# Experts of a mixture-of-experts layer: from rows kept apart and summed last, to scatters that add into one row per token

## The reference

```python
scores = sigmoid(t @ w_router)                 # 512 x 64
idx    = grouped top-8 of (scores + b_router)  # 8 experts for each token
gate   = sel / sum(sel) * 2.5
# each (token, expert) pair: rows are sorted by expert and padded to blocks
yb     = (silu(xb @ we_gate[e]) * (xb @ we_up[e])) @ we_down[e]    # D -> 256 -> D
y      = yb[dest] * gate
routed = segment_sum(y, tok)                   # the token's 8 rows are added
shared = (silu(t @ ws_gate) * (t @ ws_up)) @ ws_down
y      = routed + shared
x      = x + gt2 * rmsnorm(y, norm_ffn_post)
```

## Time and profile before

| | us |
|---|---|
| median of 3 runs | 1432.51 (1430.16 to 1439.59) |
| the profiled execution, own time | 1433.78 |
| its span, first to last instruction | 1431.9 |
| experts: first scatter to last | 680.7 to 1366.2 |
| combine: first load to end | 1380.1 to 1431.9 |

### The profile page before, as it was taken

The page is one execution under the profiler, slowest core; times in us unless marked ns, Lnnn a source line. Parts: engine busy times, 40 slices in busy tenths (PEclk is TensorE's granted clock), DMA queues, the critical chain, the costliest instruction groups (busy, mean ns, idle before and its releaser), DMA issues. The chain is left out here.

```text
span 1431.9 us, 18788 instructions
## 1 busy us (share of the span) xinstructions
PE 1314.6 (92%) x5765; PEld 912.0 (64%) x5765; DVE 1017.3 (71%) x1656; ACT 617.0 (43%) x944; POOL 254.3 (18%) x329
## 2 busy tenths in 40 slices
PE   5989999878798999986999999999999999999937
PEld 2666887637696444545767677777777676767613
DVE  4768988899633533536888888888888888887617
ACT  3421322263233103124656565665656565656402
POOL 0000000033000000002223232323232232332200
PEclk9999999988898999997999999999999999999969
DMA  9656244100004711325999999999999999988268
GB/s 331 214 206 235 67 169 147 52 22 1 1 1 184 265 59 78 157 90 213 339 343 364 351 355 353 352 344 357 382 389 351 350 342 345 362 323 322 107 239 355
DMA packets 86737, 340.80 MB, mean 238 GB/s; under 512 B 16982, under 2 KB 22296, under 8 KB 59556
## 3 DMA queue, kind: packets, MB, share of 16 engines
q1 hardware_dynamic: 66832, 306.51, 57.2%
q0 software_dynamic: 19584, 33.60, 6.4%
q10 hardware_dynamic: 276, 0.11, 0.0%
HBM read 333.87 MB, written 44.04 MB: 264 GB/s over the span
## 5 line engine op out<-in xcount | busy, mean ns | idle before, releaser
L2251 DVE TENSOR_TENSOR gate_up_low<-gate_up,gate_up_high 128x1024 fp32r<-128x1024 f32 x204 | 244.8, 1221 | 42.3 <-ACT gate_up_high L2142 36.3
L2223 PE MATMUL py<-down_ring,hT 128*128 128x512 f32 x544 | 250.0, 602 | 0.9 <-ACT hT L2161 0.9
L2184 PE MATMUL p_gate_up<-gate_up_high,x_hi 128*128 128x512 f32 x544 | 242.6, 446 | 5.3 <-DVE x_lo L2260 5.3
L2184 PE MATMUL p_gate_up<-gate_up_low,x_hi 128*128 128x512 f32 x544 | 216.8, 399 | 0.0
L2184 PE MATMUL p_gate_up<-gate_up_high,x_lo 128*128 128x512 f32 x544 | 215.7, 397 | 0.0
L2142 ACT ACTIVATE gate_up_high<-gate_up 128x1024 fp32r<-128x1024 f32 x204 | 203.6, 1051 | 0.7 <-PEq L1407 0.7
L2223 PEld LDWEIGHTS py<-down_ring,hT 128*128 128x128 f32 x544 | 98.0, 190 | 98.8 <-issue 98.7
L2184 PEld LDWEIGHTS p_gate_up<-gate_up_high,x_hi 128*128 128x128 f32 x544 | 104.0, 191 | 44.8 <-issue 21.1
L2184 PEld LDWEIGHTS p_gate_up<-gate_up_high,x_lo 128*128 128x128 f32 x544 | 103.7, 191 | 30.0 <-issue 10.9
L2113 POOL TENSOR_TENSOR carrier<-offsets 1x1 f32<-1x1 f32 x136 | 29.8, 219 | 521.6 <-DVE tokens L2269 474.1
L460 PE MATMUL pz<-h_hi,w_hi 128*128 128x512 f32 x288 | 116.9, 406 | 1.7 <-DVE ring_lo L537 1.7
(11 more groups left out here) (367 smaller groups left out, 1945.6 us busy)
## 6 DMA issues: line engine op xcount, KB each, us to landing
down_ring<-in_we_down SPq DMA_DIRECT2D x68, 1024.0 KB, 9.5
gate_up<-in_we_gate SPq DMA_DIRECT2D x51, 1024.0 KB
gate_up<-in_we_up SPq DMA_DIRECT2D x51, 1024.0 KB
ring<-in_w_ada SPq DMA_DIRECT2D x12, 2048.0 KB, 8.6
x_again<-in_we_gate SPq DMA_DIRECT2D x17, 1024.0 KB
x_again<-in_we_up SPq DMA_DIRECT2D x17, 1024.0 KB
ring<-in_w_in SPq DMA_DIRECT2D x8, 2048.0 KB, 8.3
rows<-expert_rows SPq DMA_DIRECT2D x6, 2048.0 KB, 19.0
```

The source lines that it names most:

```text
L2184: mm = pe.matmul(pgu[u % 2][:, :], x[:, u % 2, k, :], weights, start=(k == 0 and n == 0), stop=(k == KD - 1 and n == 2))
L2223: mm = pe.matmul(py[half][:, :], hT[:, u % 2, k, :], weights[:, k, half * N:half * N + N], start=(k == 0), stop=(k == 1))
L2251: V.tensor_tensor(moe.low[u % RING][:, :, piece(i), :], moe.gate_up[u % RING][:, :, piece(i), :], exact(w_hi[:, u % 2, :, piece(i), :]), A ...
```

## The change

- The scratch tensor of 4096 rows becomes `expert_sums` with one row per token (512 x 1024). At the start of the experts stage SP stores `moe.shared` (2 MB) to it.
- The scatter of each block adds to the token's row in HBM (`compute_op=ALU.add`), with the token's number as the row's number.
- Two blocks can hold the same token, so scatters go one at a time: Pool waits until scatter b-1 has landed before it issues scatter b, in every block.
- The row numbers and ranks fall away: the table has two values rather than three, `numbers` multiplies 6 columns rather than 9.
- `combine` loads 512 rows (2 MB) in four DMAs; the sums on TensorE and DVE are gone. Gate and squares work on whole tiles of 1024 columns.

```diff
@@ tabulate @@
-                for t in range(NT):
-                    link.sign(V.tensor_tensor_scan(rank[:, t, :], keep.ones[:, 0:NE], sel[:, t, :], 0.0, ALU.mult, ALU.add))
...
-                link.sign(V.tensor_tensor(rank, rank, sel, ALU.subtract))
...
-                for t in range(NT):
-                    link.sign(V.tensor_scalar(values[:, t, :, 2], rank[:, t, :], tokf[:, 2, t:t + 1], None, ALU.add))
-                link.wait()
@@ plan_experts @@
-    moe.parts = m.sb("table_parts", [P, NT, NE, 3, 3], BF16)
+    moe.parts = m.sb("table_parts", [P, NT, NE, 2, 3], BF16)
-    moe.rows = nc.dram_tensor("expert_rows", (S * TOPK, D), F32, kind="Internal").ap()
+    moe.sums = nc.dram_tensor("expert_sums", (S, D), F32, kind="Internal").ap()
@@ experts, sync @@
+            sp.wait_ge(s_x, 1)
+            sp.dma_start(moe.sums.rearrange("(t p) d -> p t d", p=P), moe.shared[:, :, :]).then_inc(s_start, 16)
             for u in range(RING):
                 weights(RING + u, u)
@@ experts, gpsimd @@
                 pool.wait_ge(s_rows, b + 1)
                 pool.wait_ge(s_yA, b + 1)
                 pool.wait_ge(s_yV, b + 1)
+                if isinstance(b, int) and b == 0:
+                    pool.wait_ge(s_start, 16)
+                else:
+                    scattered(pool, b - 1, (u + 3) % 4)
                 carry_wait(s_scatter, b, 1)
-                pool.indirect_dma_start(moe.rows, bass.IndirectOffsetOnAxis(row_ids[:, u % 4, 0:1], 0), y[:, u % 2, :], None,
-                                        bounds_check=last_row, oob_is_err=False).then_inc(s_out[u % 2], 16)
+                pool.indirect_dma_start(moe.sums, bass.IndirectOffsetOnAxis(row_ids[:, u % 4, 0:1], 0), y[:, u % 2, :], None,
+                                        bounds_check=last_token, oob_is_err=False,
+                                        compute_op=ALU.add).then_inc(s_out[u % 2], 16)
@@ experts, vector @@
-                V.tensor_tensor(row_ids[:, u % 4, :], number[:, u % 4, 2:3], moe.offsets[:, 1:2], ALU.add).then_inc(s_rows, 1)
+                V.tensor_tensor(row_ids[:, u % 4, :], number[:, u % 4, 1:2], moe.offsets[:, 0:1], ALU.add).then_inc(s_rows, 1)
@@ combine @@
+            for t in range(NT):
+                sp.dma_start(y[:, t, :], moe.sums[t * P:(t + 1) * P, :]).then_inc(s_in[t], 16)
...
+                act.activation(sq[:, :], y[:, t, :], ACT.Square, accum_out=total[:, t:t + 1]).then_inc(s_sq, 1)
+                act.wait_ge(s_sq, t + 1)
+                act.activation(mean[:, t:t + 1], total[:, t:t + 1], ACT.Copy, bias=D * RMS_EPS).then_inc(s_whole, 1)
...
+            def gated(t):
+
+                dve.wait_ge(s_in[t], 16)
+                V.scalar_tensor_tensor(out=scaled[:, t, :], in0=y[:, t, :], scalar=D ** 0.5, in1=keep.gate2[:, :],
                                        op0=ALU.mult, op1=ALU.mult).then_inc(s_gt, 1)
...
+            gated(0)
+            for t in range(NT):
+                if t + 1 < NT:
+                    gated(t + 1)
                 finish(t)
```

More of the change, by code:

```diff
@@ L1399 @@
 MAXB = NE + S * TOPK // P - 1
-NO_TOKEN, NO_ROW = 8 * S, 16 * S * TOPK
+NO_TOKEN = 8 * S
 BIG = 1e30
@@ L1433, in merge_route @@
         g8 = old(NT, NG, 8)
-        scores, biased, sel, gated, left, rank = (old(NT, NE) for _ in range(6))
-        values = old(NT, NE, 3)
+        scores, biased, sel, gated, left = (old(NT, NE) for _ in range(5))
+        values = old(NT, NE, 2)
         gs, top4, top8 = (old(NT, 8) for _ in range(3))
         gleft, gmask = old(NT, NG), old(NT, NG)
-        total, over, tokf, pf, bf = old(NT), old(NT), old(3, NT), old(1), old(4)
+        total, over, tokf, pf, bf = old(NT), old(NT), old(2, NT), old(1), old(4)
         before = old(P)
@@ L1528, in _ @@
             pool.memset(moe.offsets[:, 0:1], float(NO_TOKEN)).then_inc(s_io, 1)
-            pool.memset(moe.offsets[:, 1:2], float(NO_ROW)).then_inc(s_io, 1)
             for j in range(2 * NT):
@@ L1786, in _ @@
             link.sign(V.tensor_scalar(tokf[:, 1, :], tokf[:, 0, :], float(-NO_TOKEN), None, ALU.add))
-            link.sign(V.tensor_scalar(tokf[:, 2, :], tokf[:, 0, :], float(TOPK), float(-NO_ROW), ALU.mult, ALU.add))
             dve.wait_ge(s_x, 16)
@@ L1947, in plan_experts @@
     moe.n_blocks = m.sb("n_blocks", [1, 1], I32)
-    moe.offsets = m.sb("offsets", [P, 2])
+    moe.offsets = m.sb("offsets", [P, 1])
     moe.xg = m.sb("xg", [P, 4, D])
@@ L1978, in experts @@
         hot = m.sb("hot", [P, 2, NT, P], BF16)
-        column = m.sb("column", [P, 2, NT, 9], BF16)
-        number = m.sb("number", [P, 4, 3])
+        column = m.sb("column", [P, 2, NT, 6], BF16)
+        number = m.sb("number", [P, 4, 2])
         tokens = m.sb("tokens", [P, 4, 1], U32)
@@ L2009, in experts @@
         s_out = [m.sem(f"p5_scattered{i}") for i in range(2)]
+        s_start = m.sem("p5_sums_started")
         block = stack.enter_context(nc.Block())
@@ L2106, in _ @@
         def _(pool):
-            last_token, last_row = pool.to_reg(S - 1), pool.to_reg(S * TOPK - 1)
+            last_token = pool.to_reg(S - 1)
             def carry_wait(semaphore, b, place):
@@ L2211, in numbers @@
                 for t in range(NT):
-                    mm = pe.matmul(pid[:, 0:9], hot[:, u % 2, t, :], column[:, u % 2, t, :], start=(t == 0), stop=(t == NT - 1))
+                    mm = pe.matmul(pid[:, 0:6], hot[:, u % 2, t, :], column[:, u % 2, t, :], start=(t == 0), stop=(t == NT - 1))
                 mm.then_inc(s_id, 1)
@@ L2266, in numbers @@
                 taken(dve, s_x, b, 4)
-                V.tensor_reduce(number[:, u % 4, :], pid[:, 0:9].rearrange("p (v j) -> p v j", j=3), AX.X, ALU.add).then_inc(s_sum, 1)
+                V.tensor_reduce(number[:, u % 4, :], pid[:, 0:6].rearrange("p (v j) -> p v j", j=3), AX.X, ALU.add).then_inc(s_sum, 1)
                 dve.wait_ge(s_sum, b + 1)
@@ L2299, in combine @@
         m = Memory(nc, stack)
-        H = TOPK // 2
-        rows = m.sb("rows6", [P, NT, TOPK, D])
         x1 = moe.x1
         y, scaled = m.sb("y6", [P, NT, D]), m.sb("scaled6", [P, NT, D])
[L2304 to L2314, removed]
+        sq = m.sb("sq6", [P, D])
+        total, mean, rstd = m.sb("total6", [P, NT]), m.sb("whole6", [P, NT]), m.sb("rstd6", [P, NT])
+        s_in = [m.sem(f"p6_sums{t}_in") for t in range(NT)]
+        s_gt, s_sq, s_whole, s_r = m.sem("p6_y_gated"), m.sem("p6_squared"), m.sem("p6_squares"), m.sem("p6_rstd")
         s_o, s_st = m.sem("p6_out"), m.sem("p6_stored")
-        s_a = m.sem("p6_scalar_chain")
         block = stack.enter_context(nc.Block())
-        expert_rows = moe.rows.rearrange("(t p j) d -> t p j d", p=P, j=TOPK)
-        LAST = NT - 1
         def cols(half):
@@ L2337, in _ @@
             sp.wait_ge(s_st, 16 * 2 * NT)
[L2339 to L2348, removed]
         @block.gpsimd
@@ L2353, in _ @@
                 pool.wait_ge(s_whole, t + 1)
-                pool.tensor_tensor(rstd[:, t:t + 1], whole[:, t:t + 1], keep.power[:, 0:1], ALU.pow).then_inc(s_r, 1)
+                pool.tensor_tensor(rstd[:, t:t + 1], mean[:, t:t + 1], keep.power[:, 0:1], ALU.pow).then_inc(s_r, 1)
         @block.scalar
         def _(act):
-            link = Link(act, s_a)
             for t in range(NT):
-                act.wait_ge(s_y, 2 * t + 1)
+                act.wait_ge(s_in[t], 16)
                 if t:
[L2362 to L2368, removed]
+                    act.wait_ge(s_sq, t)
+                act.activation(sq[:, :], y[:, t, :], ACT.Square, accum_out=total[:, t:t + 1]).then_inc(s_sq, 1)
+                act.wait_ge(s_sq, t + 1)
+                act.activation(mean[:, t:t + 1], total[:, t:t + 1], ACT.Copy, bias=D * RMS_EPS).then_inc(s_whole, 1)
         @block.vector
@@ L2395, in gated @@
                                        op0=ALU.mult, op1=ALU.mult).then_inc(s_gt, 1)
             def finish(t):
+                dve.wait_ge(s_gt, t + 1)
                 dve.wait_ge(s_r, t + 1)
                 for half in range(2):
-                    dve.wait_ge(s_gt, 2 * t + half + 1)
                     V.scalar_tensor_tensor(out=x1[:, t, cols(half)], in0=scaled[:, t, cols(half)], scalar=rstd[:, t:t + 1],
                                            in1=x1[:, t, cols(half)], op0=ALU.mult, op1=ALU.add).then_inc(s_o, 1)
[L2405 to L2411, removed]
-                finish(t)
@@ L2413, in _ @@
-            for half in range(2):
-                dve.wait_ge(s_dve_in[LAST + half], 16)
-                tree(LAST, cols(half))
-                add(LAST, half)
-            for half in range(2):
-                gated(LAST, half)
-            finish(LAST)
+            gated(0)
+            for t in range(NT):
+                if t + 1 < NT:
+                    gated(t + 1)
+                finish(t)
 class Names:
```

## The result

The changed kernel took **1461.88 us** (median of 4, 1458.94 to 1473.06) against 1434.2 us for the kernel before, run beside it (median of 4): ratio 1.0205, 95% interval 1.0139 to 1.0271. It is slower by some 28 us, where 33 us less was forecast. The profiled execution took 1459.77 us, its span is 1458.0.

The account below looks back on a forecast made before the run. TensorE was taken to bound the experts, DMA close behind; loads and identity products share combine. Terms -34.1 + 0 + 0 + 0 + 1 = -33 us took 1432.5 to 1400 us, its own range 1395 to 1412, overall 1394 to 1490.

Parts of the forecast that it names:

- does the added traffic make DMA the bound: Experts loop: the add's extra 0.7 us per step on the DMA engines costs 0, at worst +9 us.
- latency L: Experts loop: time from an adding scatter's start to its landing, taken as 9.8 us; hidden if at most that.
- Part 1, combine: Combine stage: fewer loads, no identity products or DVE tree; -34.1 us, bounds -36 to -31.
- Part 2, the table: Building the table: DVE loses some 3.4 us of work, which only lengthens an idle time; 0.
- Part 3, the store: Start of experts: SP's 2 MB store of the shared rows lies in empty DMA time; 0, at worst 2 us.
- Part 4, one scatter at a time: Experts loop: Pool's wait for each scatter before the next is hidden behind TensorE's 10.35 us step; 0.
- the chain of scatters becomes the bound: Rival, experts loop: adding scatters landing after 10.9 us or more set the pace; 1453 to about 1495 us; chance 0.25.
- The slack of 9 us: Experts loop: serial scatters may fall 9.2 us behind in total before ScalarE's copy to `y` must wait.
- Lateness given back after block 60: Last 4 of 68 blocks: scatters hold only what experts have over 128 tokens, should be short and recover lateness.
- The last scatter's extra 1 us: End of experts: the last scatter lands about 1 us later and the stage's end waits for it; +1.
- the bound of -36: Combine stage: the larger gain, -36 us, if loads land in 3 us.

Follow-up runs that it names:

- without the chain: Changed kernel with two sum tensors for even and odd blocks and no wait for the scatter before, so two adding scatters may be in flight: 1455.45 us, ratio 1.0154.
- dealt kernel: Changed kernel with each block's rows permuted by the table of positions, so the first 64 fill partitions 0 to 31 and 64 to 95: 1400.18 us, ratio 0.9761.
- banded kernel: Changed kernel with the first 64 rows of a block in every second band of 16 partitions: 1471.45 us, ratio 1.0266.

## Why the prediction was wrong

Two steps failed, by one error: both count the DMA engines as one. The term "does the added traffic make DMA the bound", put at 0 and at worst +9, measured some 40 us, the part of the loop's loss that stays without the chain. The latency L of an adding scatter, put at 9.8 us, came out at 9.5 and 10.9, and the chain took another 16 us. The other terms hold: the dealt kernel took 1400.18 us, where 1400 was forecast.

**What the packets cost, against a full engine.** From the pages of the profiles: a gather or plain scatter takes 0.67 us of every engine in the mean; the adding one (0.093 x 1458.0 - 68 x 0.67) / 68 = 1.3 us, twice as much. Weights are 3.15 MB a step, 7.35 us at the peak of 428 GB/s. If all rows lie on half of the engines, those have in one step, as an estimate:

| | weights | gather | scatter | sum | measured step |
|---|---|---|---|---|---|
| before, packed | 7.35 | 1.3 | 1.3 | 10.0 | 10.35 (TensorE) |
| add, packed | 7.35 | 1.3 | 2.6 | 11.3 | 11.0 without the chain, 11.3 with it |
| add, dealt out | 7.35 | 0.7 | 1.3 | 9.4 | 10.33 (TensorE) |

The table puts the cases in order and is no proof of the 11.3. It takes the weights at the peak rate. In the mean over the engines it gives 9.4 of 10.33 us for the dealt order, a share of 0.91, where 0.98 was measured, so packets take longer than it says.

**Part 1, combine**: right. Forecast 17.7 us for the stage, measured 16.6; the first load landed after 3.4 us rather than 4.4. **Part 2, the table, and Part 3, the store**: right within what can be seen. The store landed in 8.7 us, the first scatter came at 678.0 against 680.7; over the nine kernels this start lies anywhere from 677.5 to 682.9.

**Part 4, one scatter at a time**: the value of L failed. It was put at 9.8 us, "just what fits", from a late plain scatter of 8.5 with 0.7 for the second read and 0.6 for its latency; the two in the rows above take 9.5 and 10.9. The doubling of the packets' time was forecast rightly (0.67 to 1.34). But 0.7 is a mean over 16 engines, and a scatter has landed only when the last of its 16 steps has come: in the banded kernel the first comes 4.9 us after issue, the last 10.6 (medians). The rival "the chain of scatters becomes the bound" named the sign and, with L of 10.9, 1453 us, near the 1461.88 measured; that it came so near is luck. Its mechanism is the smaller part: plain scatters in a chain are free (1396.4), adding ones without a chain are not (1455.45).

**The DMA as bound**: the working took a mean share of 0.95 and added 0.7 us to get 10.5, "at worst +9". The dealt kernel shows that the mean was not the limit (share 0.98 with TensorE at 100%). With the rows packed the same bytes held the step at 11.0 us, even without the chain. The error is to treat sixteen engines as one.

**The slack of 9 us**: it didn't help. It was counted for the copy to `y` alone, but the weights ran late as well (97 us of waits at ScalarE), and the 60 steps lost 56 us, the full 60 x 0.94.

**Lateness given back after block 60**: wrong. There Pool waits before it may issue the next gather, and the seven steps from scatter 60 to the last took 7.3 us more than before instead of less. The changed kernel's timeline at blocks 61 and 62, beside the earlier trace rows:

```profile
1368.96 2.40 POOL L2128 DMA_INDIRECT expert_sums<-y,row_ids  x1 [0.16 <-issue]
1380.57 0.51 POOL L2108 TENSOR_TENSOR carrier<-offsets 1x1 f32<-1x1 f32 x1 [9.21 <-DMA expert_sums<-y,row_ids]
...
1383.51 2.40 POOL L2128 DMA_INDIRECT expert_sums<-y,row_ids  x1 [0.16 <-issue]
1396.33 0.51 POOL L2108 TENSOR_TENSOR carrier<-offsets 1x1 f32<-1x1 f32 x1 [10.43 <-DMA expert_sums<-y,row_ids]
```

11.6 and 12.8 us, where the plain ones took 8.0 and 8.1.

**The last scatter's extra 1 us**: 0.4.

Two small slips of the working changed nothing: with the bound of -36 the sum gives 1397 us and not 1395, and an L of 10.0 gives back 0 by its own formula, not 5.

What stays open: how the remaining 16 us of the chain divide between the add's own latency and the queue behind a full engine; the dealt kernel, in which both are gone together, doesn't separate them. Nor does any run separate a full DMA engine from a full path between it and its partitions of SBUF. That the addition, which reads more from HBM and not from SBUF, is what made the difference speaks for the engine, and is only an argument.

## What to carry to other kernels

When DMAs touch only part of the partitions, ask which DMA engines they fall on, and add up the load of the fullest one, not the mean; a mean share below 1 with engines waiting for transfers is its sign. An adding scatter cost twice the engine time of a plain one here (1.3 us for 0.67). Permuting which partition holds which row cost no time in the kernel before (1432.71 for 1432.08 us), and it turned a change that lost 28 us into one that gains 32. It did lengthen Pool's own instruction for the adding scatter, from 1.59 to 2.56 us, which no engine waited for.

## What was unexpected of the hardware

- The order of the same rows over the partitions moved the time by 62 us (1461.88 to 1400.18) and the landing of unrelated weight loads from 30.3 to 8.5 us, with no change in bytes or packets.
- Waiting for each plain scatter before the next, in a stage with a DMA share of 0.95, was free (24.3 us of waits on Pool, none passed on).
- Packing into bands (1471.45) was no better than packing densely (1461.88), and there a load of weights had 12 of its 16 steps after 8.5 us and the last after 30.1.
